# Sample attention on TensorE: wide scores issued in turn for two sequences, value products in turn for four column tiles

## The chip, the cores and the metric

One core of a Trainium2 chip runs the whole program: TensorE (PE, the matrix engine, whose weight loads are shown apart as PEld), VectorE (DVE), ScalarE (ACT), GpSimd (POOL) and SyncE (SP), with SBUF, PSUM and 16 DMA engines. The metric is the device time of one execution in microseconds (us), the median of three runs.

## The reference, cut to what matters

One step of a one-layer decoder trunk, float32 throughout. Two groups of tokens share the weights: a prompt of 512 tokens, and a sample group of eight sequences with eight new tokens each. Each goes through a projection, a state-space branch and a sparse attention, a merge with a router, and a mixture of 32 experts. The change is in the attention of the sample group, where each sequence has 1024 cached rows in eight pages of 128, a window of 512 rows and its eight new rows:

```python
s_c = einsum('bqghd,bcgd->bghqc', q, kc) * scale            # 63 compressed blocks
p_c = masked_softmax(s_c, ...); o_c = einsum(..., p_c, vc)
imp_sel = ...                                               # from p_c: which blocks of 64 rows are selected
s_s = einsum('bqghd,bgqkld->bghqkl', q, k_sel) * scale      # selected rows
o_s = einsum('bghqkl,bgqkld->bqghd', softmax(s_s), v_sel)
s_w = einsum('bqghd,bkgd->bghqk', q, kw) * scale            # window rows
o_w = einsum('bghqk,bkgd->bqghd', masked_softmax(s_w, mask_w), vw)
return gate0 * o_c + gate1 * o_s + gate2 * o_w
```

## The kernel before

The program is a chain of phases with a barrier of all engines between them: `project`, `ssm_build`, `prompt`, `sample`, `merge`, `experts`, `combine`. Each phase writes one instruction list by hand for each engine; semaphores order the engines against each other, and on one engine the instructions are issued as written. The change touches only the list of TensorE in `sample`.

`sample` handles the eight sequences as four pairs, p = 0 to 3 (called first to fourth pair below). Within a pair, e = 0, 1 is the sequence and g = 0, 1 the key/value head. The 64 query rows of one sequence (2 heads g x 4 x 8 tokens) stand in `qb`; sequence e owns partitions 64e to 64e+63 of the scores in PSUM, and pair (e, g) owns the 32 partitions from lo = 64e + 32g. A matmul whose result takes 64 (or 32) partitions holds only that many columns of the 128x128 array: a column tile. The 128-row contraction uses all rows of the array, a 64-row one (the new tokens) half of them.

For a pair TensorE does, in this order:

- the wide scores (L1173 to L1181): for each sequence two 512-column matmuls against the selected keys (L1177), one 64-column matmul against the new keys (L1178), one 512-column against the window keys (L1179) and one 64-column (L1180). They go to PSUM banks 0 to 4;
- after DVE's gelu of the compression (`hid_ready`, L1182; the DVE side ends at L1313), the compressed keys and values (L1184, L1186), the compressed scores (L1191), and after the softmax of them the importance (L1195), a transpose (L1196) and the compressed value products (L1202);
- in the second and third pair, `compress` of the next pair (L1161, 32 matmuls; in the first pair it stands behind the value products instead, in the fourth there is none);
- then twice the same (`TURN`, L1207): w = 1 is the window, w = 0 the selected rows. TensorE waits for ACT's exponential (L1208, ACT's L1272), transposes the probabilities (L1215), waits for ACT's copies (L1217, ACT's L1283), and multiplies them with the values (L1230): five tiles of rows for w = 1, nine for w = 0, the last of them 64 rows high, accumulated for each (e, g) in its own 32 partitions. The window comes first; ACT's exponential of the selected rows waits for a selection chain on DVE that ends at L1357;
- DVE weighs and adds the three results (L1364 to L1367), TensorE transposes the sum (L1236), ACT copies it (L1290), and the next pair begins (L1170).

A float32 matmul leaves two records in the trace, each a weight load and a matmul, so L1230 has 40 records for w = 1 and 72 for w = 0. SP and POOL load the pages of a later pair when an earlier one ends (L1122, L1126, L1135).

Of the kernel before, what the change touches and what calls it, by code (L numbers as in the profile page):

```python
# [38 lines left out]
PAGES = PAST // PAGE  # L39
# [7 lines left out]
HD = 64  # L47
# [1005 lines left out]
def sample(nc, c):  # L1053

    with ExitStack() as ctx:
# [7 lines left out]
        pg = [Region(c.arena, AT_Z, AT_SSM).take([P, 2 * PAGES, 4, P]), region.take([P, 2 * PAGES, 4, P])]  # L1063
        wk = low.take([P, 2, 2, SEQ])
# [3 lines left out]
        kn = region.take([P, 2, 64])  # L1068
        qb = region.take([P, NB, 2, HG, NT])
# [40 lines left out]
        KT = [(1, a, P) for a in range(4)] + [(1, 4, 64)] + [(0, a, P) for a in range(PAGES)] + [(0, PAGES, 64)]  # L1110
# [7 lines left out]
        @block.sync  # L1118
        def _(sp):
            for p in range(NP):  # L1120
                if p >= 2:
                    sp.wait_ge(cmp_ps, p - 1)  # L1122

                pages(sp, p, slice(0, 2), cmp_in[p % 2], range(2 * PAGES if p else PAGES))
                if p >= 2:
                    sp.wait_ge(ot_out, 4 * (p - 1))  # L1126
                sp.dma_start(wk[:, p % 2], c.d["win_kT"][:, 2 * p:2 * p + 2]).then_inc(window_in[p % 2], 16)
                sp.dma_start(wv[:, p % 2], c.d["win_v"][:, 2 * p:2 * p + 2]).then_inc(window_in[p % 2], 16)
# [9 lines left out]
        @block.tensor  # L1138
        def _(pe):
            z4 = c.z4[0:64]  # L1140
            idn = c.k("ident")[0:64, 0:64]
            for h in range(HG):
                pe.transpose(c.ps[:, 0, h * 64:(h + 1) * 64],
                             z4[:, ZQ + h * P:ZQ + (h + 1) * P], idn)
            for s in range(2):
                pe.transpose(c.ps[:, 0, 256 + s * 64:320 + s * 64], z4[:, ZK + 256 * (s + 1):ZK + 256 * (s + 1) + P], idn)
            for p in range(NP):
                mm = pe.matmul(c.ps[:, 1, p * 24:(p + 1) * 24], c.k("expand")[0:64, p * P:(p + 1) * P], c.gate[0:64, 4],
                               start=True, stop=True)
            mm.then_inc(small_ps, 1)  # L1150
            pe.wait_ge(small_out, 3)
            pe.wait_ge(qb_zero, 9)

            def compress(p):

                pe.wait_ge(cmp_in[p % 2], 16 * 2 * PAGES * (p // 2 + 1))
                for s in range(2):
                    for g in range(2):
                        for j in range(8):
                            mov = pg[p % 2][:, :, s].rearrange("p a (g j n) -> p a g j n", g=2, j=8)[:, :, g, j]  # L1160
                            mm = pe.matmul(c.ps[:, 5, (s * 2 + g) * P:(s * 2 + g + 1) * P], c.w1[:, s, j], mov,  # L1161
                                           start=j == 0, stop=j == 7)
                mm.then_inc(cmp_ps, 1)

            for p in range(NP):
                b = p % 2
                if p == 0:
                    compress(0)
                else:
                    pe.wait_ge(ot_out, 4 * p)  # L1170
                pe.wait_ge(rest_in[b], 16 * 2 * PAGES * (p // 2 + 1))
                pe.wait_ge(window_in[b], 32 * (p // 2 + 1))
                for e in range(2):  # L1173
                    row = slice(HD * e, HD * (e + 1))
                    q = qb[:, 2 * p + e].rearrange("p g h t -> p (g h t)")
                    for a in range(2):
                        pe.matmul(c.ps[row, a, :], q, pg[b][:, e * PAGES + 4 * a:e * PAGES + 4 * a + 4, 2], start=True, stop=True)  # L1177
                    pe.matmul(c.ps[row, 2, 0:64], q, kn[:, 0], start=True, stop=True)  # L1178
                    pe.matmul(c.ps[row, 3, :], q, wk[:, b, e], start=True, stop=True)  # L1179
                    mm = pe.matmul(c.ps[row, 4, 0:64], q, kn[:, 1], start=True, stop=True)  # L1180
                mm.then_inc(wide_ps, 1)  # L1181
                pe.wait_ge(hid_ready, p + 1)  # L1182
                for g in range(2):
                    pe.matmul(c.ps[HD * g:HD * (g + 1), 6, 0:P], c.w2[:, 0], hid[:, g], start=True, stop=True)  # L1184
                    for e in range(2):
                        mm = pe.matmul(c.ps[0:63, 7, e * P + g * HD:e * P + (g + 1) * HD], hid[:, 2 + g, e * 64:e * 64 + 63],  # L1186
                                       c.w2[:, 1], start=True, stop=True)
                mm.then_inc(kc_ps, 1)
                pe.wait_ge(kc_out, 2 * p + 2)
                for e in range(2):  # L1190
                    mm = pe.matmul(c.ps[HD * e:HD * (e + 1), 5, 0:63], qb[:, 2 * p + e].rearrange("p g h t -> p (g h t)"),  # L1191
                                   kc[:, e * 64:e * 64 + 63], start=True, stop=True)
                mm.then_inc(sc_ps, 1)
                pe.wait_ge(pc_ready, p + 1)
                pe.matmul(c.ps[:, 7, 256:319], c.k("same"), pc[:, 0:63], start=True, stop=True).then_inc(imp_ps, 1)  # L1195
                pe.transpose(c.ps[0:63, 6, 0:P], pc[:, 0:63], c.k("ident")).then_inc(pct_ps, 1)  # L1196
                pe.wait_ge(pct_out, p + 1)
                pe.wait_ge(imp_out, p + 1)
                for e in range(2):
                    for g in range(2):  # L1200
                        lo = 64 * e + 32 * g
                        mm = pe.matmul(c.ps[lo:lo + 32, 7, 0:HD], pt[0:63, lo:lo + 32], vc[0:63, e, g * HD:(g + 1) * HD],  # L1202
                                       start=True, stop=True, tile_position=(0, lo))
                mm.then_inc(pv_ps, 1)
                if 0 < p < NP - 1:
                    compress(p + 1)
                for w, groups in TURN:  # L1207
                    pe.wait_ge(exp_w, 2 * p + 2 - w)  # L1208
                    for n in groups:
                        m = len(GROUPED) * p + n  # L1210
                        if m >= 2:
                            pe.wait_ge(pt_out, m - 1)
                        for a, t in enumerate(GROUPED[n]):
                            r = KT[t][2]
                            mm = pe.transpose(c.ps[0:r, BANK[n], a * P:(a + 1) * P], S[:, OFF[t]:OFF[t] + r], c.k("ident"))  # L1215
                        mm.then_inc(pt_ps, 1)
                    pe.wait_ge(pt_out, len(GROUPED) * p + groups[-1] + 1)  # L1217
                    tiles = [t for t in range(len(KT)) if KT[t][0] == w]
                    for e in range(2):
                        for g in range(2):  # L1220
                            lo = 64 * e + 32 * g
                            for t in tiles:
                                a, r = KT[t][1], KT[t][2]
                                if r == 64:
                                    v = c.z4[0:64, ZK + 256 * (w + 1) + P + g * HD:ZK + 256 * (w + 1) + P + (g + 1) * HD]
                                elif w == 0:
                                    v = pg[b][:, e * PAGES + a, 3, g * HD:(g + 1) * HD]
                                else:
                                    v = wv[:, b, e, a, g * HD:(g + 1) * HD]
                                mm = pe.matmul(c.ps[lo:lo + 32, 3 + w, 0:HD], pt[0:r, t * P + lo:t * P + lo + 32], v,  # L1230
                                               start=t == tiles[0], stop=t == tiles[-1], tile_position=(0, lo))
                    mm.then_inc(pv_ps, 1)
                if p == 0:
                    compress(1)
                pe.wait_ge(o_ready, p + 1)
                pe.transpose(c.ps[:, 2, 0:P], o[:], c.k("ident")).then_inc(ot_ps, 1)  # L1236
# [903 lines left out]
```

## Time and profile before

| what | value |
|---|---|
| median of 3 runs | 1418.52 us (1417.49 to 1420.91) |
| profiled execution: its time, its span | 1419.21 us, 1417.5 us |
| PE, DVE, ACT, POOL busy, share of the span | 83%, 30%, 24%, 20% |
| mean granted TensorE clock | 0.842 |
| sample phase on TensorE, by the timeline | from about 410 us to 569.9 us |

The span is the time from the first to the last instruction of the profiled execution. "Busy" is the time in which an engine works on at least one instruction. The granted clock is a share of TensorE's full 2.4 GHz; it stands at 1.00 or 0.50. Several matmuls of one line that follow each other are merged in the timeline into one row, with their count; a matmul's duration reaches to the end of its result, so the durations of neighbours overlap.

### The profile page before, as it was taken

Reading aid. Unit: us, or ns where it says so; the run is one execution under the profiler, and the core shown is the slowest. Engines: PE = TensorE matmul, PEld = TensorE weight load, DVE = VectorE, ACT = ScalarE, POOL = GpSimd, SP = SyncE. Lnnn points to the kernel's source line nnn. Section 1 sums busy time; section 2 is a strip of 40 time slices with the busy share of each in tenths; the row PEclk is TensorE's granted clock in tenths of the full one; section 3 lists DMA queues with packets and bytes.
Section 4 is the critical chain, followed back from the end, with each engine's and each line's share of the span. In section 5 each row is a group of like instructions: output and inputs, shape, how many; then the busy total and the mean of one; then the engine's idle time right before and its main releaser. Section 6 shows DMA issues by size and latency. Waiting matters only on the chain. (4 is left out here: it accounts for less than half of the span.)

```text
span 1417.5 us, 18752 instructions
## 1 busy us (share of the span) xinstructions
PE 1175.8 (83%) x6709; PEld 749.4 (53%) x6709; DVE 421.9 (30%) x938; ACT 336.7 (24%) x678; POOL 286.5 (20%) x702
## 2 busy tenths in 40 slices
PE   5999997788858887989999946888888888888860
PEld 5999997655536765557764443333333333333320
DVE  4437243458843333221321152100001000100005
ACT  6322122436531112120001111222212122221212
POOL 0008911288513220000000002111111112111110
PEclk9999997659887988559999957888888889888995
DMA  8321342210037420820031074999999999999935
GB/s 332 115 70 62 117 152 79 92 74 1 6 110 248 149 90 1 331 118 1 0 104 52 30 304 172 406 401 409 410 409 402 401 410 406 406 399 409 412 140 215
DMA packets 71789, 299.37 MB, mean 211 GB/s; under 512 B 12614, under 2 KB 30918, under 8 KB 45222
## 3 DMA queue, kind: packets, MB, share of 16 engines
q1 hardware_dynamic: 60734, 274.78, 49.9%
q0 software_dynamic: 9840, 22.71, 4.8%
q10 hardware_dynamic: 1152, 1.05, 0.2%
q8 instruction: 38, 0.62, 0.2%
q14 instruction: 25, 0.20, 0.0%
HBM read 284.26 MB, written 25.58 MB: 219 GB/s over the span
## 5 line engine op out<-in xcount | busy, mean ns | idle before, releaser
L1864 PE MATMUL ps<-arena,local_experts 128*64 128x512 f32 x1024 | 227.8, 596 | 2.7 <-DMA arena<-in_w_exp 1.8
L341 PE MATMUL ps<-local_project 128*128 128x288 f32 (+4 forms) x1608 | 205.1, 290 | 17.3 <-DVE local_project L480 16.6
L341 PEld LDWEIGHTS ps<-local_project 128*128 128x128 f32 (+1 forms) x1608 | 204.2, 184 | 17.8 <-DVE local_project L480 16.6
L1881 PE MATMUL ps<-arena,local_experts 128*64 128x512 f32 x512 | 176.7, 853 | 21.3 <-ACT local_experts L1903 21.3
L1921 DVE SCALAR_TENSOR_TENSOR local_experts<-local_experts,ps 64x512 f32<-64x512 f32 x32 | 21.7, 679 | 463.5 <-ACT local_experts L1899 463.5
L1864 PEld LDWEIGHTS ps<-arena,local_experts 128*64 128x64 f32 x1024 | 83.0, 138 | 144.8 <-issue 144.8
L1881 PEld LDWEIGHTS ps<-arena,local_experts 128*64 128x64 f32 x512 | 54.9, 193 | 115.9 <-issue 115.9
L1843 PE MATMUL ps<-arena,local_experts 64*128 64x64 f32 x457 | 49.7, 247 | 50.7 <-DVE local_experts L1924 42.6
L1829 POOL TENSOR_TENSOR local_experts<-local_experts 1x1 f32<-1x1 f32 x32 | 5.9, 183 | 391.6 <-ACT local_experts L1908 391.6
L1843 PEld LDWEIGHTS ps<-arena,local_experts 64*128 64x128 f32 x457 | 40.2, 162 | 81.4 <-DVE local_experts L1924 47.0
L1908 ACT ACTIVATE local_experts<-ps 64x512 f32<-64x512 f32 x64 | 37.9, 592 | 188.4 <-PE ps L1881 187.6
L1516 PE MATMUL ps<-arena 128*128 128x512 f32 (+1 forms) x160 | 71.3, 606 | 1.4 <-DVE arena L1632 1.4
L1805 POOL COPY local_experts<-arena 64x2 int32<-64x2 int32 x1 | 0.2, 177 | 332.1 <-POOLq L2050 332.1
L1899 ACT ACTIVATE local_experts<-ps 64x512 f32<-64x512 f32 x32 | 18.9, 591 | 185.4 <-PE ps L1864 185.4
L381 DVE TENSOR_TENSOR local_project<-arena,local_project 128x2048 fp32r<-128x2048 f32 (+1 forms) x15 | 35.4, 2361 | 66.3 <-ACT local_project L293 66.3
L1516 PEld LDWEIGHTS ps<-arena 128*128 128x128 f32 (+1 forms) x160 | 29.0, 183 | 41.0 <-issue 39.0
L832 PE MATMUL ps<-arena,local_prompt 128*128 128x128 f32 x160 | 29.2, 321 | 13.5 <-DVE local_prompt L992 12.9
L1797 POOL DMA_INDIRECT local_experts<-scratch_h,local_experts x34 | 33.3, 978 | 19.9 <-issue 17.6
L1473 PE MATMUL ps<-arena 64*72 64x128 f32 x128 | 36.0, 435 | 0.0
L832 PEld LDWEIGHTS ps<-arena,local_prompt 128*128 128x128 f32 x160 | 19.8, 160 | 30.2 <-DVE local_prompt L992 27.4
L1801 POOL DMA_INDIRECT scratch_rows<-local_experts x34 | 31.5, 925 | 17.8 <-issue 16.9
L924 ACT ACTIVATE local_prompt<-ps,local_prompt 128x128 f32<-128x128 f32 (+3 forms) x64 | 33.0, 521 | 8.7 <-DVE local_prompt L972 8.3
(377 smaller groups left out, 1609.5 us busy)
## 6 DMA issues: line engine op xcount, KB each, us to landing
arena<-in_w_exp SPq DMA_DIRECT2D x192, 1024.0 KB, 14.7
arena<-in_w_rest SPq DMA_DIRECT2D x9, 1024.0 KB, 5.8
arena<-in_w_wide SPq DMA_DIRECT2D x6, 1040.0 KB, 5.0
scratch_sig<-arena POOLq DMA_DIRECT2D x16, 288.0 KB, 2.5
arena<-scratch_sig SPq DMA_DIRECT2D x1, 4608.0 KB
arena<-in_x SPq DMA_DIRECT2D x2, 2048.0 KB, 8.6
arena<-in_cache POOLq DMA_DIRECT2D x32, 128.0 KB, 3.9
local_sample<-in_cache SPq DMA_DIRECT2D x32, 128.0 KB
```

The costliest lines, as they stand in the source:

```text
L341: mm = pe.matmul(out, stationary(s, k), moving(m, k), start=k == 0 and a == 0, stop=k == KD - 1 and a == 2)
L381: dve.tensor_tensor(W[:, n % 2, 1, :, 0:width], raw[:, n % 2, :, 0:width], W[:, n % 2, 0, :, 0:width].bitcast(F32), ALU.subtract).then_inc ...
L832: mm = pe.transpose(c.ps[:, 4 + g, a * P:(a + 1) * P], pr[:, ORD[u] % 3, g, a * P:(a + 1) * P], c.k("ident"))
L924: ins = act.activation(pr[:, ORD[u] % 3, g, 0:n], c.ps[:, at + g, 0:n], ACT.Exp, bias=st[:, u % 4, 1, g:g + 1], scale=SCALE, accum_out=st[ ...
L1473: mm = pe.matmul(o, c.XM[lo:lo + HD, r, tl], c.C[lo:lo + HD, r, tl].rearrange("p t e -> p (t e)"), start=False, stop=r == 1)
L1516: mm = pe.matmul(c.ps[0:ROWS[i], n, :], sig[:, k, i * P:i * P + ROWS[i]], w_out[:, k, n * 512:(n + 1) * 512], start=k == 0, stop=k == KD - 1)
L1797: pool.indirect_dma_start(X[:, q], None, c.d["h"], bass.IndirectOffsetOnAxis(ap=token[:, q].bitcast(U32), axis=0), bounds_check=TOK - 1, o ...
L1801: pool.indirect_dma_start(c.d["rows"], bass.IndirectOffsetOnAxis(ap=at.bitcast(U32), axis=0), Y[:, q], None, bounds_check=2 * TOK - 1, oob ...
L1843: return pe.transpose(out, rows, ident) if k else pe.matmul(out, rows, ident, start=True, stop=True)
L1864: mm = pe.matmul(c.ps[SLOTS * u:SLOTS * (u + 1), 2 + u, :], XT[:, 4 * half + k], raw[at + 2 * half + u][:, k], start=half == 0 and k == 0, ...
L1881: mm = pe.matmul(c.ps[SLOTS * h:SLOTS * (h + 1), 6 + h, :], HT[:, k], raw[at + 4 + h][:, k], start=k == 0, stop=k == KE - 1)
L1908: act.activation(Y[:, q, h * 512:(h + 1) * 512], c.ps[SLOTS * h:SLOTS * (h + 1), 6 + h, :], ACT.Copy).then_inc(y_out, 1)
```

## The change

The same matmuls are issued in another order; none is added, dropped or resized. The wide scores no longer go through one sequence and then the other, but change sequence with every matmul, and the 64-column ones stand last. The value products no longer finish one column tile (e, g) before the next: the loop over tiles of rows is outermost, so that four matmuls in a row go to four column tiles, and the four 64-row ones stand together at the end.

```diff
+                def query(e):
+                    return qb[:, 2 * p + e].rearrange("p g h t -> p (g h t)")
+
+                rows = [slice(HD * e, HD * (e + 1)) for e in range(2)]
+                for a in range(2):
+                    for e in range(2):
+                        pe.matmul(c.ps[rows[e], a, :], query(e), pg[b][:, e * PAGES + 4 * a:e * PAGES + 4 * a + 4, 2], start=True, stop=True)
                 for e in range(2):
-                    row = slice(HD * e, HD * (e + 1))
-                    q = qb[:, 2 * p + e].rearrange("p g h t -> p (g h t)")
-                    for a in range(2):
-                        pe.matmul(c.ps[row, a, :], q, pg[b][:, e * PAGES + 4 * a:e * PAGES + 4 * a + 4, 2], start=True, stop=True)
-                    pe.matmul(c.ps[row, 2, 0:64], q, kn[:, 0], start=True, stop=True)
-                    pe.matmul(c.ps[row, 3, :], q, wk[:, b, e], start=True, stop=True)
-                    mm = pe.matmul(c.ps[row, 4, 0:64], q, kn[:, 1], start=True, stop=True)
+                    pe.matmul(c.ps[rows[e], 3, :], query(e), wk[:, b, e], start=True, stop=True)
+                for n, bank in enumerate((2, 4)):
+                    for e in range(2):
+                        mm = pe.matmul(c.ps[rows[e], bank, 0:64], query(e), kn[:, n], start=True, stop=True)
                 mm.then_inc(wide_ps, 1)
...
                     tiles = [t for t in range(len(KT)) if KT[t][0] == w]
-                    for e in range(2):
-                        for g in range(2):
-                            lo = 64 * e + 32 * g
-                            for t in tiles:
-                                a, r = KT[t][1], KT[t][2]
+                    for t in tiles:
+                        a, r = KT[t][1], KT[t][2]
+                        for e in range(2):
+                            for g in range(2):
+                                lo = 64 * e + 32 * g
```

On TensorE the wide scores of the second pair stand before as follows, between the transpose of the first pair's result (L1236) and the compressed keys (L1184); each line is one matmul or, with a count, several of one form.

```order
L1236 MATMUL ps<-arena,local_sample 128x128
L1177 MATMUL ps<-local_sample 64x512 x2
L1178 MATMUL ps<-local_sample 64x64
L1179 MATMUL ps<-arena,local_sample 64x512
L1180 MATMUL ps<-local_sample 64x64
L1177 MATMUL ps<-local_sample 64x512 x2
L1178 MATMUL ps<-local_sample 64x64
L1179 MATMUL ps<-arena,local_sample 64x512
L1180 MATMUL ps<-local_sample 64x64
L1184 MATMUL ps<-local_sample,arena 64x128
```

And the same place now; line numbers behind L1170 are four higher from the compressed keys on (L1184 is now L1188).

```order
L1240 MATMUL ps<-arena,local_sample 128x128
L1179 MATMUL ps<-local_sample 64x512 x4
L1181 MATMUL ps<-arena,local_sample 64x512 x2
L1184 MATMUL ps<-local_sample 64x64 x4
L1188 MATMUL ps<-local_sample,arena 64x128
```

What was two runs of five matmuls, one for each sequence, is one run in which the sequences alternate. The second place is the value products of the selected rows (w = 0) of the second pair on TensorE, before: four runs of eight 128-row matmuls, each with its 64-row one, a run for each column tile.

```order
L1215 MATMUL ps<-arena,local_sample 128x128 x8
L1215 MATMUL ps<-arena,local_sample 64x128
L1230 MATMUL ps<-local_sample 32x64 x8
L1230 MATMUL ps<-arena,local_sample 32x64
L1230 MATMUL ps<-local_sample 32x64 x8
L1230 MATMUL ps<-arena,local_sample 32x64
L1230 MATMUL ps<-local_sample 32x64 x8
L1230 MATMUL ps<-arena,local_sample 32x64
L1230 MATMUL ps<-local_sample 32x64 x8
L1230 MATMUL ps<-arena,local_sample 32x64
L1236 MATMUL ps<-arena,local_sample 128x128
```

Now the rows between the transposes (L1219) and the transpose of the result (L1240) are:

```order
L1219 MATMUL ps<-arena,local_sample 128x128 x8
L1219 MATMUL ps<-arena,local_sample 64x128
L1234 MATMUL ps<-local_sample 32x64 x32
L1234 MATMUL ps<-arena,local_sample 32x64 x4
L1240 MATMUL ps<-arena,local_sample 128x128
```

The 32 matmuls with 128 rows stand together, in eight rounds over the four column tiles, and the four with 64 rows behind them. The window (w = 1) is reordered alike, with four rounds and one.

## Rows read from the trace of the kernel before

**Rows 1.** Two stages: stretch, length, busy PE PEld DVE ACT POOL, clock, DMA share, GB/s.
```profile
444.50:458.10 13.60, 10.64 (x75) 8.02 (x75) 6.80 (x23) 4.53 (x10) 2.19 (x4) 0.50 0.69 221
...
546.00:550.30 4.30, 1.69 (x19) 1.30 (x19) 2.04 (x9) 0.94 (x4) 0.00 (x0) 1.00 0.00 2
```
**Rows 2.** What TensorE waited for, 434 to 571 us: us in total, times, longest.
```profile
PE ps L1230 <- ACT local_sample L1283: 4.9, 8, 0.8
PE ps L1236 <- DVE local_sample L1367: 4.0, 3, 1.3
```
**Rows 3.** Timeline, wide scores, second and third pair: start, us, engine, line, records [idle before].
```profile
470.58 1.93 PE L1177 MATMUL ps<-local_sample 128*64 128x512 f32 x4 [0.66 <-ACT arena L1290]
...
476.01 0.43 PE L1184 MATMUL ps<-local_sample,arena 64*64 64x128 f32 x2 [0.52 <-DVEq L1313]
...
510.29 0.18 DVE L1317 TENSOR_REDUCE local_sample<-local_sample 128x3 f32<-128x24 f32 x1
...
511.22 0.43 PE L1184 MATMUL ps<-local_sample,arena 64*64 64x128 f32 x2
```
**Rows 4.** Timeline, TensorE, value products and transposes of the first, third and fourth pair.
```profile
448.71 5.43 PE L1230 MATMUL ps<-arena,local_sample 128*32 128x64 f32 x40 [0.69 <-ACT local_sample L1283]
454.06 2.22 PE L1215 MATMUL ps<-arena,local_sample 128*128 128x128 f32 x9
456.87 5.59 PE L1230 MATMUL ps<-arena,local_sample 128*32 128x64 f32 x72 [0.59 <-ACT local_sample L1283]
...
528.55 3.23 PE L1230 MATMUL ps<-arena,local_sample 128*32 128x64 f32 x40 [0.79 <-ACT local_sample L1283]
531.71 1.09 PE L1215 MATMUL ps<-arena,local_sample 128*128 128x128 f32 x8
...
533.72 5.02 PE L1230 MATMUL ps<-arena,local_sample 128*32 128x64 f32 x72 [0.36 <-ACT local_sample L1283]
...
564.50 1.08 PE L1230 MATMUL ps<-local_sample 128*32 128x64 f32 x16
...
565.74 1.08 PE L1230 MATMUL ps<-local_sample 128*32 128x64 f32 x16
```
**Rows 5.** L1230 in 528 to 540 us, grouped: records | busy, mean ns | idle before.
```profile
L1230 PE MATMUL ps<-arena,local_sample 128*32 128x64 f32 (+1 forms) x112 | 8.2, 222 | 1.2 <-ACT local_sample L1283 1.2
```
**Rows 6.** Timeline, ACT, end of the selected rows' exponential, first and third pair.
```profile
452.54 0.19 ACT L1272 ACTIVATION_READ_ACCUMULATOR local_sample<-local_sample 128x1 f32 x1
...
529.49 0.19 ACT L1272 ACTIVATION_READ_ACCUMULATOR local_sample<-local_sample 128x1 f32 x1
```
**Rows 7.** Timeline, TensorE: one column tile, two in turn, four in turn.
```profile
326.35 1.05 PE L827 MATMUL ps<-arena,local_prompt 128*32 128x128 f32 x8 [0.38 <-DVE local_prompt L985]
...
406.71 1.53 PE L859 MATMUL ps<-local_prompt,arena 128*64 128x128 f32 x24
...
446.01 0.44 PE L1202 MATMUL ps<-local_sample 63*32 63x64 f32 x8 [1.45 <-DVE local_sample L1336]
```
**Rows 8.** L1161 alone in two stretches (columns PE, PEld, clock, DMA share, GB/s).
```profile
517.00:523.00 6.00, 6.00 (x28) 6.00 (x29) 0.50 0.40 109
...
463.00:469.00 6.00, 6.00 (x56) 6.00 (x56) 1.00 0.00 0
```
**Rows 9.** Timeline, TensorE: `compress` (L1161) of three pairs, and the transpose L1196.
```profile
444.29 0.28 PE L1196 MATMUL ps<-arena,local_sample 128*63 128x128 f32 x1
...
462.40 7.41 PE L1161 MATMUL ps<-local_sample,arena 128*128 128x128 f32 x64
...
479.85 0.42 PE L1196 MATMUL ps<-arena,local_sample 128*63 128x128 f32 x1
...
481.73 9.16 PE L1161 MATMUL ps<-arena 128*128 128x128 f32 x64
...
516.94 10.28 PE L1161 MATMUL ps<-local_sample,arena 128*128 128x128 f32 x64
```
**Rows 10.** Timeline, POOL: the last page load issued for the third pair.
```profile
489.39 0.55 POOL L1106 DMA_DIRECT2D arena<-in_cache  x1 [0.61 <-issue]
```

## The prediction

> **What bounds the kernel now.** I read the view by stages first. The sample phase is a chain in which TensorE, ACT and DVE hand one pair's data to each other; nothing overlaps between pairs except `compress`. In the stretch 444.50 to 458.10 of the first pair, PE is busy for 10.64 of 13.6 us at a granted clock of 0.50 [rows 1], so half of the question is at which of the two levels (1.2 or 2.4 GHz) a matmul runs. What PE waits for says who is on the path: L1230 starts when ACT's copies end, and L1236 waits for DVE (L1367), which itself can start only after L1230 [rows 2]. So the value products stand on the path in all four pairs; in the first pair DVE's part is covered by `compress`, which PE begins directly behind L1230 [rows 4, 9]. The wide scores mostly do not: in the second pair they start at 470.58, and L1184 behind them still waits 0.52 us for DVE's gelu [rows 3]. Only in the third pair does L1184 start without an idle gap, at 511.22, when DVE had ended at 510.29 + 0.18 = 510.47 [rows 3].
>
> The later phases start behind barriers and load their weights from there, so I let them shift as they are; what the sample phase gains is gained in the end.
>
> **What alternating does to matmuls.** Three rows show it. L827 sends 8 records of 128 columns to one column tile: 1.05 us, and with 0.28 for the last one (L1196, also 128 columns [rows 9]) (1.05 - 0.28)/7 = 0.110 us from start to start. L859 sends records of 128 columns in turn to two column tiles: 24 in 1.53 us, (1.53 - 0.28)/23 = 0.054. Twice the tiles, half the spacing. L1202 sends 8 records of 64 columns to four column tiles at the lower level: 0.44 us for all [rows 7]. If the last one takes some 0.33 there (0.222 [rows 5] times the 1.5 by which L1196 grows from 0.28 to 0.42), they start about 0.02 apart. One after the other, at the 0.057 worked out below, they would take 7 x 0.057 + 0.22 = 0.62 even at the upper level. L1202 differs from the changed code in two ways, 63 rows and a burst of 8 only.
>
> **The value products, upper level.** Within one column tile 16 records take 1.08 us [rows 4], one of them 0.222 [rows 5]: (1.08 - 0.22)/15 = 0.057 from start to start. From one column tile to the next it is 565.74 - 564.50 = 1.24 us [rows 4]; the 18 records need 18 x 0.057 = 1.03, so 0.21 goes to the two changes between 128 and 64 rows. With four tiles in turn the tiles run beside each other, and the changes come once, not four times. For w = 0: 16 x 0.057 + 0.1 (one change) + 2 x 0.057 + 0.22 (the last one's end) = 1.4 us, instead of 5.02. For w = 1: 8 x 0.057 + 0.1 + 0.11 + 0.22 = 0.9 instead of 3.23 [rows 4].
>
> What comes late next: behind w = 1 the transposes L1215 need ACT's exponential of the selected rows. In the third pair that ends at 529.49 + 0.19 = 529.68 [rows 6], and PE would be done at 528.55 + 0.9 = 529.45. So L1215 moves from 531.71 to 529.7: 2.0 us, not 2.3. ACT's copies and w = 0 follow unchanged in length until L1230, which gives 5.02 - 1.4 = 3.6. Sum 5.6 us in the third pair and the same in the second, which has the same order behind its `compress`.
>
> **The value products, lower level (first and fourth pair).** I double the streams: w = 1 takes 8 x 0.114 + 0.2 + 0.23 + 0.33 = 1.7 instead of 5.43, and PE would be free at 450.4. But ACT's exponential starts only behind DVE's selection (L1357) and ends at 452.54 + 0.19 = 452.73 [rows 6], so L1215 comes forward from 454.06 to 452.8: 1.3 us; the other 2.4 are hidden by DVE and ACT. For w = 0: 16 x 0.114 + 0.2 + 0.23 + 0.33 = 2.6 instead of 5.59: 3.0. Sum 4.3 us for each of the two pairs.
>
> **The wide scores.** Now they take 476.01 - 0.52 - 470.58 = 4.9 us [rows 3]. A record of 512 columns is four of L827's 128: 0.44 us. Six of them for each sequence, beside the other's, four short ones of 0.057 and an end of 0.2 make 3.1. That is worth nothing where DVE's gelu ends later, and 511.22 - 510.5 = 0.7 us in the third pair. The reordering adds no wait and moves no DMA: SP and POOL wait for the end of pairs. Pages for the third pair are issued until 489.39 [rows 10], 15 us before that pair's first matmul; the pair would come about 10 us earlier and the issue 4, so about 9 us are left, and this cover holds.
>
> **What it costs.** TensorE's shorter bursts leave it idle longer, and the granted clock fell behind sparse stretches. Between the wide scores and the value products stand 1.69 us of small matmuls (L1184 to L1196), now at 1.00 in the fourth pair [rows 1]. With 1.8 us more of idle time ahead of them I expect the lower level there. L1196 is 0.28 at the upper level and 0.42 at the lower [rows 9], so between half of 1.69 and all of it: 0.8 to 1.7 per pair, at most 4 x 1.2 = 4.9 as my middle; the second pair is partly there already, and where `compress` starts it may come back sooner. Bounds: a loss of 6.8, and a gain of 2.4 if the denser value products lift the level in the first and fourth pair (w = 0 in 1.4 instead of 2.6, twice) and nothing else changes. I take a loss of 3.0.
>
> **The sum.** 5.6 x 2 + 4.3 x 2 + 0.7 - 3.0 = 17.5 us. The profiled execution took 1419.21 us around a span of 1417.5; 1419.2 - 17.5 = 1401.7. The median of the runs shown is 0.7 us below the profiled one, which I leave in the rounding: **1402 us**.
>
> The price not shown is four column tiles over 72 records with 128 rows. Bounds: 0.057/4 = 0.014 us per record, and 0.057, no overlap. L1202 has the same four tiles and is the nearest row, so I take the low end.
>
> Two rules speak against this value. L1202's records start about 0.02 us apart [rows 7]. The Trainium skill, TensorE: Matmul & The Clock Gate (Wait — 56ns, not 53.3ns?) says that start to start never drops below about 25 ns however few the columns. By it, as an estimate, w = 0 would take 72 x 0.025 + 0.35 = 2.2 instead of 1.4, and the whole 1403 to 1404. L859's records stand at 0.054 with weights loaded for two column tiles over the same rows [rows 7]. The Trainium skill, the same page (Part 3, The mechanism), says that a weight load overlaps running matmuls only when the row group differs, and column tiles share theirs. By that, rival 2 below would be the result; the trace does not agree, since L859 halves the spacing of L827.
>
> **Rivals.**
> 1. Only two matmuls run beside each other. For: L859 shows two with 128 rows, no row shows four over a long run. Against: L1202's burst. A record then costs 0.028: at the upper level w = 0 takes 72 x 0.028 + 0.35 = 2.4 (gain 2.6) and w = 1 1.5 (gain 1.7); at the lower level w = 0 takes 4.6 (gain 1.0) and w = 1 still hides behind ACT (1.3). 2 x 4.3 + 2 x 2.3 + 0.7 - 3 = 11: 1408 us.
> 2. The change doesn't do what it says: four tiles take turns without overlap, because loads or the queue admit one after the other. Then only the changes between 128 and 64 rows go: w = 0 72 x 0.057 + 0.35 = 4.45 (gain 0.6), w = 1 2.6 (gain 0.6), about 1.1 per pair. 4 x 1.1 less 0 to 3 of clock: about 1416 us. Against: the spacings of L859 and L1202 [rows 7].
> 3. Slower: the clock stays at its lower level through the whole phase. Place: the three `compress` blocks. There L1161 runs 28 records in 6.0 us, 64 in 13.7, instead of 7.41, 9.16 and 10.28 [rows 8, 9]: 14.2 us more. The transposes of two pairs (2 x 1.0, as nine take 2.22 where eight take 1.09 [rows 4]), w = 0 of two pairs (2 x 1.2), their w = 1, which then outlasts ACT (2 x 0.6), and the small matmuls (4.9) add 10.5. 24.7 against a gain of 20.5 makes it 4 us slower: 1423 us. It decides once the lower level holds through all three. For: 5.43 us of value products without a gap did not lift it [rows 1, 4]. Against: each dense `compress` before was granted the upper level or got it on the way [rows 8, 9].
>
> **How the numbers follow.** Forecast 68% (1396 to 1406, by the clock's bounds), rival 1 16%, rival 2 11%, rival 3 5%. The range 1397 to 1411 holds the first two and leaves out the other 16% and a little of the tails. A measurement of this kernel can tell about 0.3%, 4.3 us, from no change. Faster by more than that: the first two cases and a third of rival 2, 0.88; within it the rest of rival 2, 0.08; slower 0.04.
>
> **What would show it.** In the changed profile the 72 records of w = 0 should be one row of about 1.4 us at the upper level (2.4: rival 1; 4.4: rival 2), four starts close together. L1215 of w = 0 should wait for ACT's exponential (L1272) and not stand behind the value products. The wide scores should take 3.1 us at the upper level, with a longer wait for DVE behind them. The granted clock should read 0.50 around L1188 to L1200 in more pairs than now; if it is 0.50 through `compress`, rival 3 holds. I am wrong if the phases behind the sample phase do not keep their lengths.

## The result, and the profile after

The changed kernel takes 1397.91 us (median of 4 runs, 1394.2 to 1400.06), the kernel before 1419.72; the ratio is 0.9843 with a 95% interval of 0.9815 to 0.9872. The forecast was 1402 in a range of 1397 to 1411: right in sign and mechanism. The gain is 21.8 us instead of 17.5, and the time lies only 0.9 us above the lower end of the range.

The profiled execution has a span of 1392.5 us. Of the 25.0 us to the profile before, 4.2 lie ahead of the first wide score, in unchanged phases, and -1.4 behind the sample phase; 22.2 lie between. Executions of one kernel differ by as much: 17 runs of the kernel before on another chip went from 1410 to 1426 us.

The value products of the first and third pair on TensorE (L1234 is L1230 of before, L1219 is L1215, and so on), columns as in [rows 4]:

```profile
445.20 1.45 PE L1234 MATMUL ps<-arena,local_sample 128*32 128x64 f32 x40 [0.69 <-ACT local_sample L1287]
449.29 2.22 PE L1219 MATMUL ps<-arena,local_sample 128*128 128x128 f32 x9 [2.63 <-ACT local_sample L1276]
452.10 2.06 PE L1234 MATMUL ps<-arena,local_sample 128*32 128x64 f32 x72 [0.59 <-ACT local_sample L1287]
...
512.15 0.90 PE L1234 MATMUL ps<-arena,local_sample 128*32 128x64 f32 x40 [0.79 <-ACT local_sample L1287]
513.34 1.09 PE L1219 MATMUL ps<-arena,local_sample 128*128 128x128 f32 x8 [0.29 <-ACT local_sample L1276]
...
515.34 1.35 PE L1234 MATMUL ps<-arena,local_sample 128*32 128x64 f32 x72 [0.36 <-ACT local_sample L1287]
```

At the upper clock 72 records take 1.35 us instead of 5.02 and 40 take 0.90 instead of 3.23 [rows 4]. The transposes L1219 had no idle gap before; now they wait for L1276. ACT's timeline of the first and third pair shows the end of that exponential, as in [rows 6]:

```profile
449.05 0.19 ACT L1276 ACTIVATION_READ_ACCUMULATOR local_sample<-local_sample 128x1 f32 x1
...
513.10 0.19 ACT L1276 ACTIVATION_READ_ACCUMULATOR local_sample<-local_sample 128x1 f32 x1
```

513.10 + 0.19 = 513.29, and L1219 starts at 513.34: ACT is the next late step, as forecast. In the first pair PE idles for 2.63 us there, which is the part of the saving that DVE and ACT hide. The wide scores of the second pair, and the compressed keys of the third, as in [rows 3]:

```profile
462.27 1.94 PE L1179 MATMUL ps<-local_sample 128*64 128x512 f32 x8 [0.66 <-ACT arena L1294]
464.04 1.03 PE L1181 MATMUL ps<-arena,local_sample 128*64 128x512 f32 x4
464.89 0.40 PE L1184 MATMUL ps<-local_sample 128*64 128x64 f32 x8
467.69 0.43 PE L1188 MATMUL ps<-local_sample,arena 64*64 64x128 f32 x2 [2.40 <-DVEq L1317]
...
496.41 0.43 PE L1188 MATMUL ps<-local_sample,arena 64*64 64x128 f32 x2 [0.70 <-DVEq L1317]
```

They take 465.29 - 462.27 = 3.0 us instead of 4.9, and the wait for DVE grows from 0.52 to 2.40 us. The third pair, which had no gap there [rows 3], now has one of 0.70 us. The list of what PE waited for in the sample phase, as in [rows 2], has two new heads:

```profile
PE ps L1188 <- DVEq L1317: 6.7, 4, 2.6
PE ps L1219 <- ACT local_sample L1276: 6.3, 6, 2.6
```

The lengths of the pairs go from the first wide score of one to that of the next, the last to the end of L1236 (now L1240). Beside 470.58 [rows 3] and 462.27 above, they come from these rows, the kernel before first:

```profile
435.01 1.93 PE L1177 MATMUL ps<-arena,local_sample 128*64 128x512 f32 x4
...
504.72 2.53 PE L1177 MATMUL ps<-arena,local_sample 128*64 128x512 f32 x4 [0.66 <-ACT arena L1290]
...
541.04 1.93 PE L1177 MATMUL ps<-local_sample 128*64 128x512 f32 x4 [0.66 <-ACT arena L1290]
...
569.60 0.33 PE L1236 MATMUL ps<-arena,local_sample 128*128 128x128 f32 x1 [1.32 <-DVE local_sample L1367]
```

```profile
430.81 1.94 PE L1179 MATMUL ps<-arena,local_sample 128*64 128x512 f32 x8
...
490.99 3.52 PE L1179 MATMUL ps<-arena,local_sample 128*64 128x512 f32 x8 [0.66 <-ACT arena L1294]
...
519.03 3.35 PE L1179 MATMUL ps<-local_sample 128*64 128x512 f32 x8 [0.66 <-ACT arena L1294]
...
543.04 0.48 PE L1240 MATMUL ps<-arena,local_sample 128*128 128x128 f32 x1 [1.35 <-DVE local_sample L1371]
```

| pair | before | after | gain | w = 1 | w = 0 | wide | rest (clock) |
|---|---|---|---|---|---|---|---|
| first | 35.6 | 31.5 | 4.1 | 1.3 | 3.5 | 0 | -0.7 |
| second | 34.1 | 28.7 | 5.4 | 2.0 | 3.6 | 0 | -0.2 |
| third | 36.3 | 28.0 | 8.3 | 2.0 | 3.6 | 1.1 | 1.6 |
| fourth | 28.9 | 24.5 | 4.4 | 1.3 | 3.3 | 0 | -0.2 |

"w = 1" is the time from L1230's start to that of the next transposes, "w = 0" from L1230 to `compress` or L1236. "wide" is what L1188 comes earlier behind the first wide score (5.4 us instead of 6.5 in the third pair). The sum is 22.2 us; 21.7 of it are the three kinds of work, and 0.5 is the rest, which lies in stages where the granted level differs. This rest belongs to one execution: two more profiles of the changed sample phase, from runs below, have 113.4 and 114.2 us for the four pairs instead of 112.7, which, with the same three kinds of work, would make it -0.2 and -0.9.

### The profile page after: what moved, and what is told of

Same layout as the page of the kernel before. It is cut to its first block and busy times, and to the rows that moved or that the text cites. A ratio compares the mean times of both kernels' runs of the same rounds, so it can differ in the third digit from the quotient of the medians.

```text
span 1392.5 us, 18752 instructions
## 1 busy us (share of the span) xinstructions
PE 1129.3 (81%) x6709; PEld 719.1 (52%) x6709; DVE 422.0 (30%) x938; ACT 336.3 (24%) x678; POOL 287.9 (21%) x702
## 5 line engine op out<-in xcount | busy, mean ns | idle before, releaser
L1868 PE MATMUL ps<-arena,local_experts 128*64 128x512 f32 x1024 | 230.4, 597 | 12.2 <-DMA arena<-in_w_exp 11.2
L341 PEld LDWEIGHTS ps<-local_project 128*128 128x128 f32 (+1 forms) x1608 | 203.6, 184 | 18.1 <-DVE local_project L480 16.9
L1885 PE MATMUL ps<-arena,local_experts 128*64 128x512 f32 x512 | 165.2, 804 | 21.3 <-ACT local_experts L1907 21.3
L1925 DVE SCALAR_TENSOR_TENSOR local_experts<-local_experts,ps 64x512 f32<-64x512 f32 x32 | 21.7, 679 | 464.6 <-ACT local_experts L1903 464.6
L1477 PE MATMUL ps<-arena 64*72 64x128 f32 x128 | 36.0, 435 | 0.0
L1805 POOL DMA_INDIRECT scratch_rows<-local_experts x34 | 31.5, 926 | 17.8 <-issue 16.9
L1509 PE MATMUL ps<-local_merge 128*128 128x288 f32 x128 | 33.8, 407 | 1.3 <-DVE local_merge L1628 1.3
## 6 DMA issues: line engine op xcount, KB each, us to landing
arena<-in_w_exp SPq DMA_DIRECT2D x192, 1024.0 KB, 20.5
```

The lines of the kernel that those rows point to most:

```text
L341: mm = pe.matmul(out, stationary(s, k), moving(m, k), start=k == 0 and a == 0, stop=k == KD - 1 and a == 2)
L1477: mm = pe.matmul(o, c.XM[lo:lo + HD, r, tl], c.C[lo:lo + HD, r, tl].rearrange("p t e -> p (t e)"), start=False, stop=r == 1)
L1509: mm = pe.matmul(c.ps[:, 4 + 2 * e + u % 2, 0:HALF], w[:, k, m * P:(m + 1) * P], mov[:, k, t], start=k == 0, stop=k == 3)
L1805: pool.indirect_dma_start(c.d["rows"], bass.IndirectOffsetOnAxis(ap=at.bitcast(U32), axis=0), Y[:, q], None, bounds_check=2 * TOK - 1, oob ...
L1868: mm = pe.matmul(c.ps[SLOTS * u:SLOTS * (u + 1), 2 + u, :], XT[:, 4 * half + k], raw[at + 2 * half + u][:, k], start=half == 0 and k == 0, ...
L1885: mm = pe.matmul(c.ps[SLOTS * h:SLOTS * (h + 1), 6 + h, :], HT[:, k], raw[at + 4 + h][:, k], start=k == 0, stop=k == KE - 1)
```

## The experiments

Theory A: the gain is value products of four column tiles running beside each other, and the wide scores are hidden. Its rivals: both halves gain alike (B), only the changes between 128 and 64 rows count (C), two tiles in flight are all there is (D), and ACT does not hold back the transposes (E).

**One half alone.** First only the wide scores, then only the value products, each with its half of the diff shown above.

> Only the wide scores are reordered, the value products stay as before. Theory A (the gain is the value products running on four column tiles at once; the wide scores are hidden behind DVE's gelu): the wide scores shrink from 4.9 to 3.0 us, the wait for DVE behind them grows from 0.5 to 2.5 us, and only the third pair gains, about 1 us, while the first may lose 0.7 us to a lower granted clock in L1188 to L1200; in all 0 to 1 us faster, no difference that can be measured. Theory B (both halves of the change gain): 7 to 8 us faster, 1.9 us per pair.

Measured: 1417.16 us, ratio 0.9998 (0.9979 to 1.0017). In its profile, third pair:

```profile
506.30 1.94 PE L1179 MATMUL ps<-arena,local_sample 128*64 128x512 f32 x8 [0.66 <-ACT arena L1294]
...
508.93 0.40 PE L1184 MATMUL ps<-local_sample 128*64 128x64 f32 x8
511.73 0.43 PE L1188 MATMUL ps<-local_sample,arena 64*64 64x128 f32 x2 [2.40 <-DVEq L1317]
```

The scores take 509.33 - 506.30 = 3.0 us, and L1188 comes 5.4 us behind the first of them instead of 6.5: this pair gains 1.1 us. In the second pair, where they took 4.9, the 1.9 us saved only lengthen the wait for DVE. B falls, since the interval leaves at most 3 us. The profile shows too what the clock of a single execution does: its four pairs take 130.1 us, 4.9 less than in the profile before. Only 1.1 of that is the wide scores; most of the rest is a level that rose earlier in the first and fourth pair, and the time of the runs is no better for it.

> Only the value products are reordered, the wide scores stay as before. Theory A: all of the gain, 20 to 22 us, ratio 0.985; the first pair's L1184 to L1196 stay at the upper clock (0.7 us better than in the whole change), the third pair's wide scores end about 1 us behind DVE's gelu. Theory B: 13 to 14 us.

Measured: 1400.42 us, ratio 0.9880 (0.9858 to 0.9902), a gain of 18 us: most of it, a little under the 20 to 22 that A expected. The end of the second pair shows what is gained, the third and fourth pair what stays without the wide scores' half:

```profile
492.40 1.10 PE L1230 MATMUL ps<-local_sample 128*32 128x64 f32 x64 [0.36 <-ACT local_sample L1283]
493.43 0.32 PE L1230 MATMUL ps<-arena,local_sample 64*32 64x64 f32 x8
...
496.09 3.43 PE L1177 MATMUL ps<-arena,local_sample 128*64 128x512 f32 x4 [0.66 <-ACT arena L1290]
...
499.53 0.72 PE L1179 MATMUL ps<-arena,local_sample 128*64 128x512 f32 x1
499.53 0.75 PE L1177 MATMUL ps<-arena,local_sample 128*64 128x512 f32 x1
...
502.59 0.43 PE L1184 MATMUL ps<-local_sample,arena 64*64 64x128 f32 x2
...
526.36 3.00 PE L1177 MATMUL ps<-local_sample 128*64 128x512 f32 x4 [0.66 <-ACT arena L1290]
...
532.86 0.43 PE L1184 MATMUL ps<-local_sample,arena 64*64 64x128 f32 x2
```

64 records take 1.10 us, (1.10 - 0.22)/63 = 0.014 from start to start. And L1184 comes 6.5 us behind the first wide score, without a gap, where the whole change has 5.4: in that pair the wide scores, partly at the lower clock, are late by 1.1 us. In this execution the fourth pair shows the same 6.5 us, where before it had a gap of 0.5. So the wide scores' half, worth nothing that can be measured alone, is worth some 2 us here on top of the other half.

**Only the 64-row matmuls moved to the end**, column tile by column tile otherwise:

```diff
-                    for e in range(2):
-                        for g in range(2):
-                            lo = 64 * e + 32 * g
-                            for t in tiles:
+                    last = tiles[-1:]
+                    for ts, e, g in [(ts, e, g) for ts in (tiles[:-1], last) for e in range(2) for g in range(2)]:
+                        lo = 64 * e + 32 * g
...
+                            for t in ts:
```

> The value products go column tile by column tile as before, but the four 64-row matmuls stand together at the end, so that the array changes between 128 and 64 rows once instead of four times; the wide scores stay as before. Theory A: w = 0 takes 3.9 to 4.5 us at the upper clock instead of 5.02, the gain is 5 to 8 us. Theory C (the gain comes from the changes between 128 and 64 rows, not from tiles running beside each other): nearly the whole gain, 18 us or more.

Measured: 1404.83 us, ratio 0.9913 (0.9891 to 0.9935), 13.7 us faster: more than A allowed, less than C. In the third pair:

```profile
519.93 1.64 PE L1231 MATMUL ps<-arena,local_sample 128*32 128x64 f32 x40 [0.79 <-ACT local_sample L1284]
...
523.50 3.43 PE L1231 MATMUL ps<-arena,local_sample 128*32 128x64 f32 x72 [0.36 <-ACT local_sample L1284]
```

3.43 us, 1.0 less than 72 records one behind the other and one change (4.45). The records' starts in that trace tell why: at each of the three joints the first four records of the next column tile start between the last four of the one before (at the first joint 0.694, 0.700, 0.750, 0.780, 0.806, 0.836 us and so on, counted from the first record's start). That saves 3 x 4 x 0.056 = 0.7, and the eight 64-row records, now on four tiles in a row, run packed, 0.3. The same is seen in the rows of the run with only the value products reordered: the second sequence's first L1177 starts at 499.53 together with L1179 of the first sequence, which has four records left then. So in these traces a run on one column tile holds back the next until four of its records are left, and the old order had no such joint: its last two records had 64 rows, and the next tile's first record started 0.15 us behind the last of them. A had not foreseen this.

For the time it means, by the medians, that 13.7 of the 18.1 us that the value products gain on this chip come with the 64-row matmuls moved alone; going through four tiles in turn adds the other 4. The rows at the upper clock say why: w = 1 falls from 3.23 to 1.64 and then to 0.90 us, but ACT's exponential hides all below 1.2, and w = 0 falls from 5.02 to 3.43 and then to 1.35.

**Two column tiles in turn**, the two sequences, one head after the other, 64-row matmuls last:

```diff
...
+                    last = tiles[-1:]
+                    for ts, g in [(ts, g) for ts in (tiles[:-1], last) for g in range(2)]:
+                        for t in ts:
+                            a, r = KT[t][1], KT[t][2]
+                            for e in range(2):
...
```

> The value products alternate between two column tiles (the two sequences) and go through the two heads one after the other, 64-row matmuls at the end; the wide scores stay as before. Theory A: a record starts every 0.028 us at the upper clock; w = 0 takes 2.4 us, w = 1 1.5 us, the gain is 13 us (4.3 in the second and third pair, 2.3 in the first and fourth). Theory D (two tiles in flight are all that the array takes): the same times as the whole change, w = 0 1.35 us, gain 21 us.

Measured: 1400.77 us, ratio 0.9879 (0.9856 to 0.9903), 17.7 us faster.

```profile
518.21 1.15 PE L1231 MATMUL ps<-arena,local_sample 128*32 128x64 f32 x40 [0.79 <-ACT local_sample L1284]
...
521.40 2.04 PE L1231 MATMUL ps<-arena,local_sample 128*32 128x64 f32 x72 [0.36 <-ACT local_sample L1284]
```

The 2.04 us lie nearer A's 2.4 (the joint again) than D's 1.35: four tiles do run beside each other. It is this row that decides, not the time: 17.7 us lie between A's 13 and D's 21, and the run with four tiles in turn and the same wide scores took 1400.42 us, no different from this one's 1400.77. By the rows two tiles should be some 3 us short of four, all of it in w = 0, since w = 1 at 1.15 us is already hidden by ACT's exponential; the two intervals, about 3 us to either side, can't show that.

**The change once more**, without an edit, beside the runs that build on it.

> The changed kernel itself, timed beside the others on one chip. Theory A: ratio 0.984 to 0.986 to the kernel before, as in its first measurement, and in the profile 72 records of w = 0 in 1.35 us at the upper clock and 2.0 to 2.3 us at the lower.

Measured: 1397.02 us, ratio 0.9851 (0.9822 to 0.9881): the first result again, and the number that the next runs are held against.

**Window's value products back in the old order**, everything else changed, to measure what ACT hides.

> The changed kernel with the window's value products (w = 1) back in the old order, column tile by column tile; those of the selected rows (w = 0) and the wide scores stay changed. Theory A with ACT's exponential as the next late step: w = 1 takes 3.23 us (upper clock) or 5.43 us (lower) again, of which 2.0 us in the second and third pair and 1.3 us in the first and fourth are seen at the start of the transposes for w = 0, 6.6 us slower than the changed kernel in all, gain 15 us against the kernel before. Theory E (ACT's exponential does not hold back the transposes, PE's own work is what counts): 2.33 us and 3.98 us per pair, 12.6 us slower than the changed kernel, gain 9 us.

Measured: 1405.62 us, ratio 0.9896 (0.9860 to 0.9933); beside it the whole change with 1397.02. First and third pair:

```profile
447.60 5.43 PE L1236 MATMUL ps<-arena,local_sample 128*32 128x64 f32 x40 [0.69 <-ACT local_sample L1289]
452.96 2.23 PE L1219 MATMUL ps<-arena,local_sample 128*128 128x128 f32 x9
...
520.24 3.23 PE L1236 MATMUL ps<-arena,local_sample 128*32 128x64 f32 x40 [0.79 <-ACT local_sample L1289]
523.40 1.09 PE L1219 MATMUL ps<-arena,local_sample 128*128 128x128 f32 x8
```

From L1236 to the transposes it is 5.36 and 3.16 us, against 4.09 and 1.19 in the changed kernel: 1.3 and 2.0 more, A's terms, not E's 4.0 and 2.3. Its 8.6 us over the change lie between A's 6.6 and E's 12.6, and the intervals of both ratios are 4 to 5 us wide to either side; the profile, not the time, decides for A.

**Filling the new gap.** The 2.6 us in which PE waits for L1276 suggest putting `compress` there, in the first three pairs:

```diff
-                if 0 < p < NP - 1:
-                    compress(p + 1)
...
+                    if w == 1 and p < NP - 1:
+                        compress(p + 1)
                     pe.wait_ge(pt_out, len(GROUPED) * p + groups[-1] + 1)
...
-                if p == 0:
-                    compress(1)
```

> The changed kernel with compress of the next pair moved, in the first three pairs, behind the window's transposes and ahead of its value products, where PE now waits for ACT's copies; in the first pair it stood behind the value products. If PE's own work bounds these pairs: about 2.4 us faster than the changed kernel in the first pair and 0.5 us in each of the second and third, 3 to 4 us in all. If the exponential of the selected rows bounds them: no gain beyond 1 us.

Measured: 1390.86 us, ratio 0.9804 (0.9770 to 0.9837), 6 us faster than the change in the medians of one chip, though the two intervals overlap. First pair:

```profile
446.36 8.32 PE L1161 MATMUL ps<-local_sample,arena 128*128 128x128 f32 x64
454.61 0.90 PE L1234 MATMUL ps<-arena,local_sample 128*32 128x64 f32 x40
455.44 1.09 PE L1217 MATMUL ps<-arena,local_sample 128*128 128x128 f32 x8
...
457.44 1.35 PE L1234 MATMUL ps<-arena,local_sample 128*32 128x64 f32 x72 [0.36 <-ACT local_sample L1285]
```

No wait is left ahead of the window's value products or for the exponential; 0.36 us for the copies of the selected rows stays. The value products of this pair now run at the upper clock (0.90 and 1.35 instead of 1.45 and 2.06). The pair takes 27.6 us instead of 31.5. Against the profile of the change on the same chip the first three pairs are 3.7, 1.2 and 2.3 us shorter, where 2.4, 0.5 and 0.5 were expected. Both expectations were too low. Part of the surplus is the clock: `compress` of the third pair takes 8.3 us here and 10.2 there.

**The same thought elsewhere.** In merge a 128-row product (L1475) and two 64-row ones (L1477) follow each other for each of 32 state groups, all at the lower clock. The edit takes two groups in turn, whose 64-row products use different halves of the array's rows:

```diff
-            for n in range(NY):
-                if n >= 4:
-                    pe.wait_ge(y_done, n - 3)
+            for n0 in range(0, NY, 2):
+                if n0 >= 4:
+                    pe.wait_ge(y_done, n0 - 2)
...
                 for a in range(4):
...
+                    for n in (n0, n0 + 1):
...
+                        pe.matmul(o, c.U[:, g], ..., start=True, stop=False)
                     for r in range(2):
...
+                        for n in (n0, n0 + 1):
...
+                            mm = pe.matmul(o, c.XM[lo:lo + HD, r, tl], ..., start=False, stop=r == 1)
...
```

> The changed kernel, and the same thought in the next phase: the first product of merge (L1475 with 128 rows, L1477 twice with 64) takes two state groups in turn, so that the 64-row matmuls alternate between the lower and the upper half of the array's rows and the changes between 128 and 64 rows are halved. Theory A carried over: two groups take 2.2 us instead of 3.4 at the lower clock, 12 to 18 us faster than the changed kernel. If only the changes of rows count and row halves do not run beside each other: 5 to 7 us faster.

Measured: 1376.56 us, ratio 0.9698 (0.9666 to 0.9730), 20.5 us faster than the change. The changed kernel first, one state group and the start of the next, then the edit, two groups and two more:

```profile
545.08 0.67 PE L1475 MATMUL ps<-arena 128*72 128x128 f32 x2 [1.56 <-PEq L2054]
545.68 1.13 PE L1477 MATMUL ps<-arena 64*72 64x128 f32 x4
546.73 0.70 PE L1475 MATMUL ps<-arena 128*72 128x128 f32 x2
```

```profile
550.02 1.10 PE L1479 MATMUL ps<-arena 128*72 128x128 f32 x4 [1.56 <-PEq L2062]
551.05 1.13 PE L1484 MATMUL ps<-arena 64*72 64x128 f32 x8
552.11 1.13 PE L1479 MATMUL ps<-arena 128*72 128x128 f32 x4
...
565.22 0.66 PE L1479 MATMUL ps<-arena 128*72 128x128 f32 x4 [2.91 <-DVE local_merge L1627]
```

Eight 64-row records take the 1.13 us that four took, and two groups 552.11 - 550.02 = 2.1 us instead of 3.4. Halved changes of rows alone would not give this, so the row halves do run beside each other, and the gain lies above the 12 to 18 us that A expected. The whole product shrinks from 54.0 to 31.8 us in the profiles. At 2.1 us throughout it would be some 34; part of it now runs at the upper level (0.66 us for four records), and twice PE waits 2.91 us for DVE, the next late step here.

**Both further edits together.**

> The changed kernel with both further edits: compress of the next pair inside the window's part (6 us faster than the change when alone) and the first product of merge in turn on the two halves of the array's rows (20 us faster when alone). The two stand in different phases behind a barrier, so the gains should add: about 1371 us, ratio 0.966 to the kernel before. If the granted clock or the transfers of merge eat one of them: 1376 us or more.

Measured: 1374.32 us, ratio 0.9685 (0.9672 to 0.9698), the fastest here. It falls between the two expectations; the profiled execution keeps both gains (the sample phase ends 107 us behind the first wide score, 112.7 in the change, and the merge product takes 31.7 us). Where the other 3 us of the median went is open; the ratio with the merge edit alone is 0.9698 (0.9666 to 0.9730), so `compress` is not shown to add to it in time, though the sample phase keeps its shorter length in the profile.

## Why the prediction was right, point by point

- **The path.** Value products on it in all four pairs: the two halves alone show it (ratio 0.9998 and 0.9880). Wide scores only in the third, 1.1 us (0.7 forecast): so in the profile before. With the value products reordered alone the fourth pair joined it, which the sum did not foresee.
- **Four tiles run beside each other.** Forecast 1.4 and 0.9 us for w = 0 and w = 1 at the upper clock, measured 1.35 and 0.90. At the lower clock 2.6 and 1.7 were forecast. w = 1 took 1.45; w = 0 took 2.06 in the first pair, where the level rose on its way, and 543.04 - 1.35 - 539.39 = 2.30 in the fourth, where it stayed:

```profile
539.39 1.93 PE L1234 MATMUL ps<-local_sample 128*32 128x64 f32 x64 [0.59 <-ACT local_sample L1287]
```

0.057 doubled was a little too much: in the profile before, records of w = 1 at the lower level start 0.107 us apart, and a change of rows adds 0.13 there, not 0.2. The forecast put the gain down to the tiles in turn with the changes counted once; in time the moved 64-row matmuls are the larger part of it (13.7 of 18.1 us).
- **The two rules of the Trainium skill** (TensorE: Matmul & The Clock Gate). The section Wait — 56ns, not 53.3ns? states a floor of about 25 ns from start to start; the 64 records here start 14 ns apart. Part 3, The mechanism, lists weight loads as overlapping running matmuls only in another row group, though it also lets them go ahead into a background weight buffer; these share their row group and run four abreast. For column tiles in turn the measurement decides against both sentences.
- **What is late next.** L1219 waits for L1276, and comes forward by 1.3 and 2.0 us per pair as forecast; the window's value products put back gave the same terms.
- **The step that was mis-sized: the clock's cost.** I forecast a loss of 3.0 us; the profiles have between a gain of 0.5 and a loss of 0.9. It is the larger part of the 4.3 us by which the forecast missed. (4 x 1.2 is also 4.8 and not 4.9, which moves nothing.) I expected the longer idle time behind the wide scores to lower the clock for L1188 to L1200 in most pairs. In this execution it did so in the first only, at 0.7 us; the stages show it, columns as in [rows 1]:

```profile
436.60:441.50 4.90, 2.68 (x19) 2.01 (x18) 1.97 (x9) 0.98 (x5) 2.46 (x5) 0.50 1.01 365
467.60:470.70 3.10, 1.22 (x16) 0.95 (x16) 0.89 (x5) 0.94 (x4) 1.13 (x3) 1.00 0.88 269
496.30:500.40 4.10, 1.77 (x19) 1.30 (x19) 1.84 (x10) 1.00 (x5) 1.81 (x4) 1.00 0.36 120
524.40:528.40 4.00, 1.77 (x19) 1.30 (x19) 1.78 (x9) 0.95 (x5) 0.00 (x0) 1.00 0.01 2
```

In the third and fourth pair the level had fallen during the wide scores instead (in the third it had done so before as well), which were then 4.7 and 4.4 us long, but still under DVE's cover. `compress` of the third pair took 8.7 us instead of 10.28 [rows 9], which makes the 0.5 a gain. The change did not bring this: the changed kernel run once more has the old length, here the profile after and then that run:

```profile
502.12 8.70 PE L1161 MATMUL ps<-local_sample,arena 128*128 128x128 f32 x64
```

```profile
500.63 10.23 PE L1161 MATMUL ps<-local_sample,arena 128*128 128x128 f32 x64
```

So the clock cost about nothing, give or take 1 us, and why the level stands where it does in one execution and not in another is open. The rest of the sum, 20.5 us before the clock, came out as 21.7.
- **Rival 2's price** was wrong as well: without tiles in turn, and only the changes of rows gone, it gave some 4 us; the run with the 64-row matmuls last gained 13.7, since neighbouring tiles overlap at their joints and the 64-row records run packed. That run is thus not rival 2 itself, which allowed no overlap.

## What to carry to other kernels

In these traces narrow matmuls on different column tiles, or on different halves of the rows, run beside each other only as far as the instruction order lets them meet: put matmuls of different tiles next to each other, and keep those of one row count together. The second alone gave three quarters of the value products' gain here. Look for it where TensorE is dense and waits for nothing: here one loop order in another phase gave as much as this change. Before counting the saving, find who is late next (here an exponential behind a DVE chain leaves only 1.3 of some 4 us of the window's saving at the lower clock, and 2.0 of 2.33 at the upper) and whether the shorter work was on the path at all. And do not read a gain or a cost of the clock from one profile: the same sample phase differed by 1.5 us over three profiles, and one stage of it by as much.

## What the runs showed of the hardware that was not expected

- Within 64 records, four column tiles take a record every 0.014 us, a weight load and a matmul each. Each tile keeps its own pace of 0.056, and the records of the four tiles start 0.007 us apart (at the upper level in the third pair: 515.422, .429, .435, .442, then .478), so there the bound is the tile and not the issue.
- A run of 10 or 16 records on one column tile lets the next tile begin when four of its records are left. With two 64-row records at its end nothing of the next tile starts between them, and each change between 128 and 64 rows costs about 0.1 us at the upper clock: 0.15 us from start to start instead of 0.056.
- Where the level rises in the first pair does not go with the order of the value products. Before, it stayed at 0.50 through the 5.43 us of w = 1 [rows 1, 4] and rose within w = 0, column tile by column tile (0.50 from 456.87 to 457.50, 0.94 from 457.50 to 462.40). With only the wide scores reordered it rose at the end of w = 1 in the same old order (0.50 from 451.60 to 456.50, 1.00 from 456.80 to 463.80). In the changed kernel it rose within w = 0 again, the four tiles in turn (0.50 from 452.10 to 453.40, 0.82 from 453.40 to 454.10).
